# Moving the modulation products of the FFN loops from TensorE to ScalarE and GpSimd

## What is computed

```python
for layer in range(DEPTH):
    mod = (silu(c) @ w_ada[layer] + b_ada[layer]).reshape(..., N_MOD, 1, D_MODEL)      # 1024 x 9216
    mod_c = (silu(c_ctx) @ w_ada[layer] + b_ada[layer]).reshape(N_MOD, 1, D_MODEL)
    lm, cm = nine vectors of 1024 each, of mod and of mod_c
    h = h + 0.5 * lm[2] * swiglu(modulate(rms_norm(h, norm_w[layer, 0]), lm[0], lm[1]), w_in0, w_out0)
    # the same for the context with cm; then token_mix with lm[3..5], a second FFN with lm[6..8]
def swiglu(h, w_in, w_out):                   # D_FF = 2816
    gate, up = jnp.split(h @ w_in, 2, axis=-1)
    return (jax.nn.silu(gate) * up) @ w_out
```

## Time and profile before

| | us |
|---|---|
| median of 3 executions | 2952.94 (2949.46 to 2954.81) |
| span of the profiled execution | 2948.6 |
| TensorE busy in it | 2846.3 (97%) |
| VectorE busy | 1117.0 (38%) |
| ScalarE busy | 756.4 (26%) |
| GpSimd busy | 198.8 (7%) |

### The profile page before, as it was taken

One profiled execution on the slowest core, in us unless ns is written; L12 is line 12 of the kernel. 1 busy time (PEld: TensorE's weight loads), 2 busy tenths in 40 slices (PEclk: granted clock), 3 DMA queues, 4 the chain that ended last, 5 costly groups with the idle time before them and its releaser, 6 DMA issues.

```text
span 2948.6 us, 41048 instructions
## 1 busy us (share of the span) xinstructions
PE 2846.3 (97%) x16339; PEld 2367.4 (80%) x16339; DVE 1117.0 (38%) x1663; ACT 756.4 (26%) x1167; POOL 198.8 (7%) x151
## 2 busy tenths in 40 slices
PE   6999999999999989999999899999998999899998
PEld 4888888878749878888888788888886848788887
DVE  5222222344468452222233522222235457543333
ACT  4111111132337231111111411111123246422222
POOL 2000000020041020000000200000002041100000
PEclk9999999999999999999999999999998999999999
DMA  6433233313200133422222234333432300133332
GB/s 219 130 114 95 84 114 114 95 49 93 57 1 2 36 93 114 119 74 57 64 72 71 84 113 119 98 93 114 119 102 79 78 22 1 57 93 104 88 101 91
DMA packets 414110, 252.19 MB, mean 86 GB/s; under 512 B 24445, under 2 KB 409809, under 8 KB 414033
## 3 DMA queue, kind: packets, MB, share of 16 engines
q1 hardware_dynamic: 414032, 251.16, 28.9%
HBM read 249.03 MB, written 2.10 MB: 85 GB/s over the span
## 4 chain that ended last, share of the span: by engine, by line
PE 91%; DVE 5%; ACT 2%; issue 1%; DMA 1%; SPq 1%; ACTq 0%; DVEq 0%
PE pg L619 75%; PE pg L696 4%; PE p L635 2%; PE p L905 2%; DVE xlo L1429 2%; PE pn L889 1%; DVE xhi L1428 1%; PE p L835 1%; PE p L644 1%; PE pg L835 1%; PE pg L858 1%; DVE wlo L1310 0%; ACT xfull L1080 0%; PE pn L780 0%; PE pg L780 0%
## 5 line engine op out<-in xcount | busy, mean ns | idle before, releaser
L619 PE MATMUL pg<-xhi,whi 128*128 128x512 f32 x2880 | 808.0, 349 | 8.4 <-DVE wlo L1310 6.4
L619 PE MATMUL pg<-xhi,wlo 128*128 128x512 f32 x2880 | 803.1, 347 | 0.0
L619 PE MATMUL pg<-xlo,whi 128*128 128x512 f32 x2880 | 799.3, 346 | 0.0
L1002 ACT CAST whi<-raw 128x1024 fp32r<-128x1024 f32 (+1 forms) x288 | 321.5, 1117 | 1135.4 <-PE pg L619 1132.3
L1310 DVE TENSOR_TENSOR wlo<-raw,whi 128x1024 fp32r<-128x1024 f32 (+1 forms) x288 | 382.4, 1328 | 586.2 <-ACT whi L1002 583.7
L619 PEld LDWEIGHTS pg<-xhi,whi 128*128 128x128 f32 x2880 | 456.8, 189 | 100.3 <-issue 23.6
L619 PEld LDWEIGHTS pg<-xhi,wlo 128*128 128x128 f32 x2880 | 456.9, 189 | 70.8
L619 PEld LDWEIGHTS pg<-xlo,whi 128*128 128x128 f32 x2880 | 455.1, 188 | 71.3
L619 PE MATMUL pg<-ahi,whi 128*128 128x512 f32 x1100 | 306.6, 347 | 0.0
L619 PE MATMUL pg<-alo,whi 128*128 128x512 f32 x1100 | 305.2, 345 | 0.0
L619 PE MATMUL pg<-ahi,wlo 128*128 128x512 f32 x1100 | 304.3, 344 | 0.0
(11 more groups left out here) (201 smaller groups left out, 2349.9 us busy)
## 6 DMA issues: line engine op xcount, KB each, us to landing
raw<-in_ffn_w_in SPq DMA_DIRECT2D x176, 512.0 KB, 3.9
ada<-in_w_ada SPq DMA_DIRECT2D x128, 512.0 KB, 4.4
raw<-in_ffn_w_out SPq DMA_DIRECT2D x64, 704.0 KB, 4.6
raw<-in_w_in SPq DMA_DIRECT2D x24, 512.0 KB, 4.0
ada_first<-in_w_ada SPq DMA_DIRECT2D x8, 1024.0 KB, 11.8
dft_sb<-in_dft SPq DMA_DIRECT2D x2, 2048.0 KB, 9.9
raw<-in_w_in SPq DMA_DIRECT2D x16, 256.0 KB, 3.5
raw<-in_w_o SPq DMA_DIRECT2D x16, 256.0 KB, 2.8
```

What stands on the lines that cost most here:

```text
L619: last = nc.tensor.matmul(pg[s][:, p0:p1], w[:, s, k], v[:, k, p0:p1], start=(k == 0 and n == 0), stop=(k == kt - 1 and n == 2))
L1002: nc.scalar.copy(whi[:, s, 0:nk], raw[:, s, 0:nk]).then_inc(s_whi[s], 1)
```

## The change

Sixteen tiles of 128 partitions take the place of eight products. Each pair's 1024 rows of `w_ada` are loaded as four pieces of four tiles; a tile has 64 rows, and holds them twice, in partitions 0 to 63 and again in 64 to 127. ScalarE multiplies each tile in place by a column of `cond2`, which has SiLU of `c` in partitions 0 to 63 and of `c_ctx` in 64 to 127 (`scale_ada`). GpSimd adds the 16 tiles one after the other into `part`, each addition behind a wait for the one before (`sum_ada`). TensorE's fold stays, with `halves`, which sums the two halves of the partitions apart. The pieces 0 and 1 lie where `ada` was; the pieces 2 and 3 lie in the region `m` behind `gate`, where `tnorm` and `xfull` are during a norm, so the first loads behind a norm wait for its end. `ADA_PAIRS` is another table: 62 pairs in "in" steps and 2 in "out" steps, where it was 55 and 9.

```diff
@@ -52,8 +52,11 @@
...
-ADA_PAIRS = {(0, 0, 0): (16, 11, 1), (0, 0, 1): (40, 11, 1), (0, 1, 0): (64, 11, 1),
-             (1, 0, 0): (88, 11, 3), (1, 0, 1): (116, 11, 3)}
+ADA_PAIRS = {(0, 0, 0): (16, 11, 2), (0, 0, 1): (42, 11, 0), (0, 1, 0): (64, 11, 0),
+             (0, 1, 1): (86, 11, 0), (1, 0, 0): (108, 11, 0), (1, 0, 1): (130, 7, 0)}
+ADA_PIECES = 4
+ADA_TILES = 2 * KD
+ADA_ADDS = ADA_TILES - 1
@@ -126,7 +129,10 @@
...
-        ada = place("ada", [P, 2, KD // 2, 2 * P], f32, start["ada"])
+        ada = [place(f"ada{q}", [P, ADA_TILES // ADA_PIECES, 2 * P], f32, at) for q, at in enumerate(
+            (start["ada"], start["ada"] + 4096, start["m"] + 2 * TOK * 4, start["m"] + 2 * TOK * 4 + 4096))]
@@ -406,6 +414,10 @@
...
+        def sum_value(t, i):
+            return i * ADA_ADDS + ADA_ADDS * ((t - ADA_FIRST) // 2)
@@ -454,15 +466,20 @@
...
-            def load_ada(t, i, layer):
-                for b in range(2):
+            def load_ada(t, i, layer, norm_done):
+                c0 = (t - layer * MT) * P
+                for q in range(ADA_PIECES):
+                    if q == 2 and norm_done is not None:
+                        sp.wait_ge(s_xn, norm_done)
                     if not (isinstance(i, int) and t + 2 * i == ADA_FIRST):
-                        sp.wait_ge(s_ada_used, i * 2 + (t + b - ADA_FIRST - 1))
-                    c0 = (t - layer * MT) * P
-                    sp.dma_start(ada[:, b], w_ada[layer][D // 2 * b:D // 2 * (b + 1), ds(i * (2 * P) + c0, 2 * P)
-                                                         ].rearrange("(k p) n -> p k n", p=P)).then_inc(s_ada[b], 16)
+                        sp.wait_ge(s_sum, sum_value(t, i) + (4 * (q + 1) - ADA_TILES))
+                    rows_ = D // ADA_PIECES
+                    for v in range(2):
+                        sp.dma_start(ada[q][HD * v:HD * v + HD], w_ada[layer][
+                            rows_ * q:rows_ * (q + 1), ds(i * (2 * P) + c0, 2 * P)].rearrange("(k p) n -> p k n", p=HD)
+                                     ).then_inc(s_ada[q], 16)
...
+                            load_ada(b, f, layer, xn_count(m, 1, KD - 1) if isinstance(f, int) and not hf else None)
...
-                            load_ada(b, 0, layer)
+                            load_ada(b, 0, layer, xn_count(m, 1, KD - 1))
+                            a = 1
+                        elif kind == "in" and hf == 0 and a == 0:
+                            load_step(0, b, layer)
                             a = 1
                         with sp.Fori(a, e) as j:
                             load_step(j, b, layer)
@@ -579,9 +599,33 @@
...
+            def sum_ada(t, i, q):
+                pool.wait_ge(s_mul, i * ADA_PIECES + (2 * (t - ADA_FIRST) + q + 1))
+                for a in range(ADA_TILES // ADA_PIECES):
+                    n = q * (ADA_TILES // ADA_PIECES) + a
+                    if n == 0:
+                        pool.wait_ge(s_fold, i + (t - ADA_FIRST) // 2)
+                    elif n == 1:
+                        nc.gpsimd.tensor_tensor(part[:, :], ada[q][:, 0], ada[q][:, 1], ALU.add).then_inc(s_sum, 1)
+                    else:
+                        pool.wait_ge(s_sum, sum_value(t, i) + n - 1)
+                        nc.gpsimd.tensor_tensor(part[:, :], part[:, :], ada[q][:, a], ALU.add).then_inc(s_sum, 1)
+            def ada_sums(m):
+                for i in range(len(phases)):
+                    if phases[i][0] in ("in", "out") and phases[i][2] == m:
+                        for a, e, b, _ in ada_runs(i, phases[i][4] // 2):
+                            if b is not None:
+                                with pool.Fori(a, e) as f:
+                                    for q in range(ADA_PIECES):
+                                        sum_ada(b, f, q)
...
             for l in range(DEPTH):
                 tq = TOK if l < DEPTH - 1 else SEQ
                 norm(3 * l)
+                ada_sums(3 * l)
...
+                ada_sums(3 * l + 2)
@@ -626,22 +671,12 @@
...
-            def ada_product(t, i):
-                for b in range(2):
-                    pe.wait_ge(s_ada[b], i * 16 + (8 * (t - ADA_FIRST) + 16))
-                    for j in range(4):
-                        last = nc.tensor.matmul(pa[0][32 * j:32 * j + 32, 0:2 * P], cond[:, 4 * b + j], ada[:, b, j],
-                                                start=(b == 0), stop=(b == 1))
-                    last.then_inc(s_ada_used, 1)
             def ada_fold(t, i):
-                pe.wait_ge(s_part, i + ((t - ADA_FIRST) // 2 + 1))
+                pe.wait_ge(s_sum, sum_value(t, i) + ADA_ADDS)
                 pe.wait_ge(s_mod, i + t // 2)
                 for b in range(2):
-                    last = nc.tensor.matmul(pa[1][:, 2 * b:2 * b + 2], part[:, b * P:(b + 1) * P], fold,
+                    last = nc.tensor.matmul(pa[1][:, 2 * b:2 * b + 2], part[:, b * P:(b + 1) * P], halves,
                                             start=True, stop=True)
                 last.then_inc(s_fold, 1)
@@ -929,13 +964,10 @@
                         if hf == 0 and a == 0:
                             first_pair(i, t)
                             if b is not None:
-                                ada_product(b, 0)
                                 ada_fold(b, 0)
                             a = 1
                         with pe.Fori(a, e) as f:
                             unit(i, 0, f, xhi, xlo, t)
-                            if b is not None:
-                                ada_product(b, f)
                             unit(i, 1, f, xhi, xlo, t)
                             if b is not None:
                                 ada_fold(b, f)
@@ -1022,16 +1052,24 @@
...
-            def copy_part(t, i):
-                act.wait_ge(s_ada_used, i * 2 + (t - ADA_FIRST + 2))
-                nc.scalar.copy(part[:, :], pa[0][:, 0:2 * P]).then_inc(s_part, 1)
+            def scale_ada(t, i, q):
+                act.wait_ge(s_ada[q], i * 32 + (16 * (t - ADA_FIRST) + 32))
+                for a in range(ADA_TILES // ADA_PIECES):
+                    n = q * (ADA_TILES // ADA_PIECES) + a
+                    last = nc.scalar.mul(ada[q][:, a], ada[q][:, a], cond2[:, n:n + 1])
+                last.then_inc(s_mul, 1)
...
+            for v in range(2):
+                for b in range(2):
+                    nc.scalar.activation(cond2[HD * v:HD * v + HD, b::2], vecs[HD * b:HD * b + HD,
+                                                                               48 + KD * v:48 + KD * v + KD], ACT.Silu
+                                         ).then_inc(s_cond, 1)
@@ -1230,6 +1269,9 @@
                 if kind == "in":
                     def step(f, nxt, jn, b):
+                        if b is not None:
+                            scale_ada(b, f, 0)
+                            scale_ada(b, f, 1)
                         act.wait_ge(s_unit[0], f + (j0 + 1))
                         if hf or not isinstance(f, int) or f:
                             if isinstance(f, int) and f == 0:
@@ -1239,7 +1281,8 @@
                         nc.scalar.activation(gate[:, 0:t], pg[0][:, 0:t], ACT.Silu).then_inc(s_free[0], 1)
                         split_hi(nxt, 0, jn)
                         if b is not None:
-                            copy_part(b, f)
+                            scale_ada(b, f, 2)
+                            scale_ada(b, f, 3)
                         split_hi(nxt, 1, jn)
@@ -1252,10 +1295,11 @@
                 elif kind in ("out", "wo"):
                     def step(j, nxt, jn, b):
                         for s in range(2):
+                            if b is not None:
+                                scale_ada(b, j, 2 * s)
+                                scale_ada(b, j, 2 * s + 1)
                             if nxt < len(phases):
                                 split_hi(nxt, s, jn)
-                            if b is not None and s == 0:
-                                copy_part(b, j)
                             if next_norm(i) is not None:
```

More of the change, by code:

```diff
@@ L73, in constants @@
         np.block([[c64, z], [z, c64]]), np.block([[s64, z], [z, s64]]),
-        np.tile(np.eye(32)[:, :2], (4, 1))], axis=1)
+        np.tile(np.eye(32)[:, :2], (4, 1)), np.repeat(np.eye(2), HD, axis=0)], axis=1)
     window = np.concatenate([np.where(k >= q, 0.0, NEG), np.where(k <= q, 0.0, NEG)], axis=1)
@@ L180, in transformer @@
         junk = place("junk", [P, D], f32, x0 + 3 * D * 4)
-        consts = sb("consts", [P, 5 * P + 2])
+        consts = sb("consts", [P, 5 * P + 4])
         fold = consts[:, 5 * P:5 * P + 2]
+        halves = consts[:, 5 * P + 2:5 * P + 4]
         ident_r = sb("ident_r", [P, P], f32r)
@@ L223, in transformer @@
         s_free = [sem(f"psum_read{s}") for s in range(2)]
-        s_ada = [sem(f"ada_loaded{s}") for s in range(2)]
+        s_ada = [sem(f"ada_loaded{q}") for q in range(ADA_PIECES)]
         s_ada0 = [sem(f"ada_first_loaded{q}") for q in range(4)]
@@ L490, in load_step @@
```

(6 more changed lines are left out.)

6 lines of the change are left out of this document (4 added, 2 removed).

## The result

| | before | after |
|---|---|---|
| median, us (4 executions each) | 2951.32 (2949.46 to 2954.81) | 3134.93 (3127.39 to 3137.35) |
| ratio, 95% interval | | 1.0613 (1.0597 to 1.0629) |
| span of the profiled execution | 2948.6 | 3134.2 |
| mean granted TensorE clock of it | 0.987 | 0.948 |

The account below looks back on a forecast made before the run. TensorE, busy for 97% of 2948.6 us, was taken to bound the kernel. First steps +30, other "in" steps 145.1 against 94.1, "out" steps 1.5 against 16.5: +66 on the 2952.94 median, 3019 us, range 2970 to 3110.

Follow-up runs that it names:

- experiments 1 and 8: 1: changed kernel with piece 2 scaled ahead of SiLU too, 2940.05 us; 8: the same with no pair in the three first steps behind a norm, 2887.69 us.

## What to carry to other kernels

Before work is moved off TensorE, ask what its next instruction in line will wait for, and price that wait as its length, some 0.45 us to get going again, and, where it is longer than the 1.08 us that never cost the clock here, up to 1.6 us for the clock. How often that is paid depends on where the waits lie, so both ends belong in the range. A chain over slower engines belongs early in the step, so that its last link is done when TensorE comes by: moving four scalings ahead of one wait turned +6.1% into -0.4%, and sparing the three steps where the chain can't start early made it -2.3%. Where a granted clock in a window is below 1.00 in the kernel before, look at what TensorE did ahead of it; it is a first price for a new wait.

## What the runs showed of the hardware

- Waits of TensorE once a step of about 20 us: at 0.87 to 1.08 us the clock fell in 0 of 103 steps, at 1.54 in 2 of 47, at 1.72 in 23 of 47, at 1.61 to 1.80 (in the changed kernel) in 40 of 53. At the ends of phases 1.22 us had no fall in two cases, 1.36 had one in three. A fall is to 0.50 (1.2 GHz) for some 3.4 us and costs 1.54 us in the changed kernel. A half of the time at the lower clock lost, and a fall paid once for each wait, is also what the Trainium skill, "TensorE: Matmul & The Clock Gate", section "HAM oscillation — how this bites in real kernels", describes; the waits it speaks of are longer than those that sufficed here.
- Equal waits had unequal outcomes, and the place of the wait tells them apart: in the changed kernel the fold at 171.54 waited 1.62 us and the step behind it has a fall (20.88), the fold at 213.37 waited 1.62 as well and its step has none (19.44); the first wait starts at 0.23 of the beat on which the clock changes, the second at 0.48. Of 147 waits of 1.54 to 1.80 us all 65 that start from 0.88 over the beat to 0.44 have a fall, and none of the 82 others. This is read from the traces and not tested: no run shifts a wait along the beat with its length held.
- A chain of GpSimd additions, each waiting for the one before, costs 0.06 to 0.08 us a link over the 0.737 of the addition.
- Also open: the doubled reading of `w_ada` was never tried by itself. The steps of experiments 1 and 8 have it, at a DMA share of 0.69 to 0.75, and TensorE does not wait in them.
